# Output projection of the second layer as seven products of half matrices, with left sums on VectorE and right sums on GpSimd

## The reference

```python
        else:
            h = x @ b_w_in[j]
            u, v, qm = jnp.split(h, [SGU_WIDTH, 2 * SGU_WIDTH], axis=-1)
            mix = causal_chunk_sgu(jax.nn.gelu(u), jax.nn.gelu(v), sgu_ln_g[j], sgu_ln_b[j],
                                   sgu_w_s[j], sgu_b_s[j])
        mo = memory_attention(qm.reshape(B, S, N_MEM_HEADS, HEAD_DIM), mk, mv).reshape(B, S, MEM_WIDTH)
        y = jnp.concatenate([mix, mo], axis=-1) @ w_out[i]
        x = layer_norm(DN_ALPHA * x + y, ln_mix_g[i], ln_mix_b[i])
        f = (jax.nn.silu(x @ w_gate[i]) * (x @ w_up[i])) @ w_down[i]
        x = layer_norm(DN_ALPHA * x + f, ln_ffn_g[i], ln_ffn_b[i])
```

## Time and profile before

| what | value |
|---|---|
| median of 3 runs | 2175.58 us (2175.55 to 2175.66) |
| profiled execution: its span, first to last instruction | 2173.8 us |
| what the runs' time has beyond that span | 1.8 us |
| TensorE busy / weight loads | 99% / 84% of the span |
| VectorE, ScalarE, GpSimd busy | 62%, 43%, 60% |
| mean granted TensorE clock | 0.997 of full |

### The profile page before, as it was taken

How to read it: one execution, slowest core, us unless ns; L and a number is a source line. 1 busy time by engine, 2 the same in 40 slices (tenths; PEclk the granted TensorE clock), 3 DMA queues, 4 the chain that set the end, 5 groups by cost and what they waited for, 6 DMA issues and landing times.

```text
span 2173.8 us, 32211 instructions
## 1 busy us (share of the span) xinstructions
PE 2143.0 (99%) x10960; PEld 1822.5 (84%) x10960; DVE 1343.5 (62%) x2447; ACT 929.9 (43%) x1751; POOL 1301.1 (60%) x863
## 2 busy tenths in 40 slices
PE   8999999999999999999999999999999999999997
PEld 7888888888888888888888899988878888888885
DVE  5655565655875555566547747657866555555567
ACT  5655555632533343443324753213444333333323
POOL 5221222374498777777773793424698777777764
PEclk9999999999999999999999999999999999999998
DMA  5211111142012111111131311201012111111111
GB/s 176 74 53 46 58 49 59 44 136 59 20 59 59 58 51 55 54 51 55 46 96 49 102 48 47 78 22 57 20 59 68 55 57 54 58 58 58 54 62 79
DMA packets 164701, 132.64 MB, mean 61 GB/s; under 512 B 12656, under 2 KB 148464, under 8 KB 164592
## 3 DMA queue, kind: packets, MB, share of 16 engines
q1 hardware_dynamic: 149568, 115.36, 17.6%
q10 hardware_dynamic: 15024, 15.83, 2.5%
HBM read 122.78 MB, written 4.19 MB: 58 GB/s over the span
## 4 chain that ended last, share of the span: by engine, by line
PE 91%; DVE 4%; POOL 3%; issue 1%; ACT 1%; DMA 0%; ACTq 0%; DVEq 0%; POOLq 0%
PE ps L361 27%; PE ps L363 27%; PE ps L362 27%; PE ps L716 3%; PE ps L744 2%; PE ps L745 2%; PE ps L703 2%; PE ps L704 1%; POOL Rl L1896 1%; PE ps L1149 1%; POOL XR L1333 1%; PE ps L1063 1%; DVE V L2418 1%; POOL raw L1918 0%; DVE T2l L1606 0%
## 5 line engine op out<-in xcount | busy, mean ns | idle before, releaser
L2102 DVE TENSOR_TENSOR XR<-XR,ps 128x512 f32<-128x512 f32 x504 | 338.8, 686 | 215.4 <-PE ps L363 215.4
L318 POOL TENSOR_TENSOR Wh<-raw,zcol 128x1024 fp32r<-128x1024 f32 x76 | 144.7, 1904 | 466.6 <-PE ps L363 389.5
L1896 POOL TENSOR_TENSOR Rl<-raw,Rh 128x512 fp32r<-128x512 f32 x216 | 285.6, 1324 | 121.4 <-ACT Rh L1740 118.9
L361 PE MATMUL ps<-XTh,Wh 128*128 128x512 f32 x608 | 248.6, 409 | 0.5 <-DVE bQl L922 0.4
L363 PE MATMUL ps<-XTh,Wl 128*128 128x512 f32 x608 | 238.2, 392 | 0.0
L362 PE MATMUL ps<-XTl,Wh 128*128 128x512 f32 x608 | 237.8, 391 | 0.0
L361 PE MATMUL ps<-XTh,Rh 128*128 128x512 f32 x576 | 224.3, 389 | 3.3 <-POOL Rl L1896 3.3
L362 PE MATMUL ps<-XTl,Rh 128*128 128x512 f32 x576 | 224.1, 389 | 0.0
L363 PE MATMUL ps<-XTh,Rl 128*128 128x512 f32 x576 | 224.1, 389 | 0.0
L1740 ACT ACTIVATE Rh<-raw 128x512 fp32r<-128x512 f32 x216 | 135.8, 630 | 167.7 <-PE ps L363 143.6
L361 PE MATMUL ps<-Wh,XTh 128*128 128x256 f32 (+1 forms) x576 | 192.0, 333 | 0.0
(11 more groups left out here) (302 smaller groups left out, 5572.4 us busy)
## 6 DMA issues: line engine op xcount, KB each, us to landing
raw<-in_w_up SPq DMA_DIRECT2D x44, 512.0 KB, 3.8
raw<-in_w_gate SPq DMA_DIRECT2D x72, 256.0 KB, 2.9
rows<-in_w_down SPq DMA_DIRECT2D x36, 512.0 KB, 3.7
raw<-in_a_w_in SPq DMA_DIRECT2D x20, 512.0 KB, 3.8
raw<-in_w_out SPq DMA_DIRECT2D x16, 512.0 KB, 3.7
raw<-in_b_w_in SPq DMA_DIRECT2D x15, 512.0 KB, 3.8
B<-in_c_bias SPq DMA_DIRECT2D x12, 512.0 KB, 3.7
raw<-in_w_mem_kv SPq DMA_DIRECT2D x8, 512.0 KB, 3.9
```

The costliest lines, as they stand in the source:

```text
L318: nc.gpsimd.tensor_tensor(high, raw[:, turn, :], zcol[:, 0:1].to_broadcast([P, UNIT]), ALU.add).then_inc(high_done, 1)
L361: nc.tensor.matmul(dst, wh, xh, start=first, stop=False, skip_group_check=onto)
L1896: nc.gpsimd.tensor_tensor(Rl[(w - 1) % 4][:, :], source(w), Rh[(w - 1) % 4][:, :].bitcast(F32), ALU.subtract).then_inc(gs[L]("low"), 1)
L2102: nc.vector.tensor_tensor(x, x, bank(4 + i), ALU.add).then_inc(gf[L]("added"), 1)
```

## The change

The 1024x1024 times 1024x1024 product is cut in halves in each direction and made as seven products of halves (Winograd's form) instead of eight. The left matrix needs four sums, S1 to S4, of quarters of the activations; the right one four, T1 to T4, of quarters of `w_out`. Each quarter is stored as two pieces (`c` = 0, 1) of 128x1024 values per partition row, so each sum is two instructions, and so are its high part and its low part.

```diff
+    BLOCKS = [(b, c) for b in ("11", "12", "22") for c in range(2)]
+    BLOCKS = [BLOCKS[n] for n in (0, 1, 2, 4, 3, 5)]
...
+    PLACE = ((0, 1), (1, 1), (0, 1), (0, 0), (1, 0), (1, 1), (0, 1))
+    OPENS = (0, 1, 5)
+    FIRST_BANK = (0, 4, 0, 0, 0, 4, 4)
+    TO = ((1, 0), (1, 0), (1, 1), (0, 1), (0, 0), (0, 1), (1, 1))
+    LEFT_SUMS = [(n, c) for c in range(2) for n in ("S3", "S1", "S2")] + [("S4", c) for c in range(2)]
+    LEFT_OF = {2: "S2", 3: "S3", 5: "S1", 6: "S4"}
+    SUM_OF = {2: "T2", 3: "T3", 4: "T4", 5: "T1"}
...
+    def seven_pe(pe, d, units=range(4)):
...
+        for i in units:
+            b = FIRST_BANK[d] + i
...
+            else:
+                pe.wait_ge(*go[1]("added", 4 * {2: 0, 3: 2, 4: 3, 5: 1, 6: 5}[d] + i + 1))
...
+            for c in range(2):
+                if i == 0:
+                    pe.wait_ge(*right_split("low", d, c))
+                    if d in LEFT_OF:
+                        pe.wait_ge(*left_split("low", LEFT_OF[d], c))
+                rh, rl = right_of(d, c)
+                for k in range(2):
...
+                    mm = three(bank(b), XTh[:, at_k, ts], XTl[:, at_k, ts], rh[:, k * 512:k * 512 + 512],
+                               rl[:, k * 512:k * 512 + 512], opens and (c, k) == (0, 0), (c, k) == (1, 1), onto=not opens)
+            mm.then_inc(go[1]("product"), 1)
...
+    def left_high7_act(act, n, c):
...
+        nc.scalar.activation(left_place(XTh, d, c), left_source7(n, c), ACT.Copy).then_inc(g7("left_high"), 1)
...
+    def right_sum7_pool(pool, n, c):
...
+        nc.gpsimd.tensor_tensor(dst, x, y, op).then_inc(g7("right_sum"), 1)
+    def right_high7_act(act, d, c):
...
+        if d < 3:
+            act.wait_ge(sem("uproj_product"), (2 * NT, 3 * NT, NT)[d])
+        else:
+            act.wait_ge(*go[1]("product", 4 * (d - 2)))
...
+    def seven_pool(pool):
+        for c in range(2):
+            right_low7_pool(pool, 0, c)
+        for n, c in RIGHT_SUMS[:4]:
+            right_sum7_pool(pool, n, c)
+        for d in (1, 2):
+            for c in range(2):
+                right_low7_pool(pool, d, c)
+        for c in range(2):
+            right_sum7_pool(pool, "T4", c)
+        for c in range(2):
+            right_low7_pool(pool, 3, c)
+        for c in range(2):
+            right_sum7_pool(pool, "T1", c)
+        for d in (4, 5, 6):
+            for c in range(2):
+                right_low7_pool(pool, d, c)
...
+    def seven_sums_dve(dve):
+        for n, c in LEFT_SUMS[:6]:
+            left_sum7_dve(dve, n, c)
+        for c in range(2):
+            left_low7_dve(dve, "S2", c)
+        seven_dve(dve, 0, range(2, 4))
+        for c in range(2):
+            left_low7_dve(dve, "S3", c)
+        seven_dve(dve, 1)
+        for c in range(2):
+            left_low7_dve(dve, "S1", c)
+        for n, c in LEFT_SUMS[6:]:
+            left_sum7_dve(dve, n, c)
+        seven_dve(dve, 2)
...
+    def tile_at(n):
+        return (n + 4) % NT
...
         for n in range(7, 3 * NT):
             gelu(n)
+            if n == 2 * NT + 1:
+                for c in range(2):
+                    right_high7_act(act, 0, c)
             if n >= 2 * NT + 2:
                 turn(n - 2 * NT - 2)
-        turn(NT - 2)
-        turn(NT - 1)
+        for d in (1, 2):
+            for c in range(2):
+                right_high7_act(act, d, c)
+            turn(NT - 3 + d)
...
+            else:
+                seven_pe(pe, 0, range(2, 4))
+                for d in range(1, 6):
+                    seven_pe(pe, d)
+                seven_pe(pe, 6, range(2))
+                for j in range(4):
+                    row_turn(pe, go[1], j, None)
+                seven_pe(pe, 6, range(2, 4))
```

More of the change, by code:

```diff
@@ L254, in build, with part_of @@
     VSLOTS = (6, 7, 0, 1, 2, 3)
[L255 to L261, removed]
+    OUT_PARTS = [(0, 1, 2), (3, 4, 5), (6, 7)]
+    CLOSE = len(OUT_PARTS) - 1
+    def part_of(k):
+        return next(c for c, ks in enumerate(OUT_PARTS) if k in ks)
     def letters(p):
@@ new lines, in build, with summed, left_summed, left_split @@
+    LEFT_OF = {2: "S2", 3: "S3", 5: "S1", 6: "S4"}
+    RIGHT_SUMS = [(n, c) for c in range(2) for n in ("T3", "T2")] + [(n, c) for n in ("T4", "T1") for c in range(2)]
+    SUM_OF = {2: "T2", 3: "T3", 4: "T4", 5: "T1"}
+    B_OF = ("11", "21", "11", "12", "21", "12", "22")
+    def summed(t, h):
+        d = (1, 6)[h] if t >= 4 else (4, 5)[h]
+        return go[1]("added", 4 * d + t % 4 + 1)
+    def left_summed(n, c):
+        return g7("left_sum", LEFT_SUMS.index((n, c)) + 1)
+    def left_split(part, n, c):
+        return g7(f"left_{part}", LEFT_SPLITS.index((n, c)) + 1)
@@ new lines, in right_summed, with right_split, block_f32, block_landed @@
+    def right_summed(n, c):
+        return g7("right_sum", RIGHT_SUMS.index((n, c)) + 1)
+    def right_split(part, d, c):
+        if d == 4:
+            return {"high": high_done, "low": split_done}[part], U_B21 + c + 1
+        return g7(f"right_{part}", 2 * (d - (d > 4)) + c + 1)
+    def block_f32(b, c):
+        return raw[:, (U_B21 + c) % RS, :] if b == "21" else blocks_f32[b, c][:, :]
+    def block_landed(b, c):
+        if b == "21":
+            return raw_landed[(U_B21 + c) % RS], 16 * ((U_B21 + c) // RS + 1)
+        return BLOCK_LANDED[b, c]
@@ new lines, in seven_dve @@
+    def seven_dve(dve, d, units=range(4)):
+        row, half = TO[d]
+        for i in units:
+            dve.wait_ge(*go[1]("product", 4 * d + i + 1))
+            x = XR[:, 4 * row + i, half * 512:half * 512 + 512]
+            p = bank(FIRST_BANK[d] + i)
+            if d in FIRST_TOUCH:
+                nc.vector.scalar_tensor_tensor(x, x, ALPHA, p, ALU.mult, ALU.add).then_inc(go[1]("added"), 1)
+            else:
+                dve.wait_ge(*go[1]("added", 4 * TO.index(TO[d]) + i + 1))
+                nc.vector.tensor_tensor(x, x, p, ALU.add).then_inc(go[1]("added"), 1)
@@ new lines, in seven_norm_dve @@
+    def seven_norm_dve(dve):
+        g = go[1]
+        for i in range(4):
+            seven_dve(dve, 5, (i,))
+            if i:
+                rstd_dve(dve, g, i - 1)
+            stats_dve(dve, g, None, i, range(1, 2))
+        seven_dve(dve, 6, (0,))
+        rstd_dve(dve, g, 3)
+        stats_dve(dve, g, None, 4, range(1, 2))
+        rstd_dve(dve, g, 4)
+        seven_dve(dve, 6, (1,))
+        for j in range(2):
+            row_dve(dve, g, j)
+        seven_dve(dve, 6, (2,))
+        for j in range(2, 4):
+            row_dve(dve, g, j)
+        stats_dve(dve, g, None, 5, range(1, 2))
+        seven_dve(dve, 6, (3,))
+        rstd_dve(dve, g, 5)
+        for j in range(4, KT):
+            row_dve(dve, g, j)
+        stats_dve(dve, g, None, 6, range(1, 2))
+        stats_dve(dve, g, None, 7, range(1, 2))
+        rstd_dve(dve, g, 6)
+        rstd_dve(dve, g, 7)
@@ L2212, in ready @@
                 pe.wait_ge(sem("mix_low"), (3, 5, 7)[c])
[L2213 to L2220, removed]
+        acc_pe(pe, go[0], c, U_OUT + ks[0], lambda i, t: out_lhs(ks[i], t), [out_rhs(k) for k in ks], ready,
+               after=norm_pe_after(pe, go[0], c) if c == CLOSE else None, tiles=tiles, halves=halves)
     def out_piece_pe(pe, n, k):
         t, h = n // 2, n % 2
-        pe.wait_ge(split_done, U_OUT[0] + k + 1)
+        pe.wait_ge(split_done, U_OUT + k + 1)
         pe.wait_ge(sem("mix_low"), k + 1)
@@ L2688, in _ @@
         pool.wait_ge(*gsg("v_low", NG))
-        for u in range(U_U + 4, U_FFN[1]):
+        for u in range(U_U + 4, U_B21):
             split(pool, u)
+        seven_pool(pool)
         ffn_units(1)
@@ L2749, in _ @@
                 sgu_pe(pe)
[L2751 to L2752 removed]
+            if L == 0:
+                for c in range(len(OUT_PARTS)):
+                    out_pe(pe, c, range(3, NT) if c == 0 else range(NT))
+            else:
+                seven_pe(pe, 0, range(2, 4))
[5 more added lines that the diff above has]
+                seven_pe(pe, 6, range(2, 4))
+                for j in (4, 5):
+                    row_turn(pe, go[1], j, None)
             ffn_pe(pe, L, 0, True, False)
```

290 lines of the change are left out of this document (216 added, 74 removed).

## The result

The changed kernel takes 2185.45 us (median of 4 runs, 2184.27 to 2185.56), the kernel before 2175.62 us (4 runs) on the same chip. The ratio is 1.0044, with a 95% interval of 1.0031 to 1.0056: slower by 9.8 us. The forecast was 2185.8 us, in a range of 2171 to 2192.

What follows compares the result with a forecast made beforehand. The prediction took TensorE, busy 99% of the span, as the bound. Its terms, -10.9 + 4.0 + 2.3 + 12.4 + 0.5 + 1.9 = +10.2 us, gave 2185.8 us, in a range of 2171 to 2192.

Steps and rivals of the forecast that it cites:

- Matmuls, -10.9: Second output projection: 384 matmuls become 336, and the 48 removed save 0.2267 us each on PE, -10.9 us.
- A pair costs 3.35: One POOL and one DVE instruction of 128x1024, both reading SBUF, largely take turns: 3.35 us together, between 2.38 and 3.52.
- Turns, +4.0: Turns of U tiles before the projection: DVE's short SBUF instructions wait out six POOL instructions over three tiles, +4.0 us.
- Before d2, +2.3: Ahead of product d2: DVE's left sums meet three POOL instructions, so S2's first low part comes late, +2.3 us.
- Before d3, +12.4: Ahead of product d3: DVE's addition of d2 stands behind five instructions that each meet one of POOL's, +12.4 us.
- Before d4, +0.5: Ahead of product d4: DVE's addition of d3 is queued behind S4's low parts and four statistics, +0.5 us.
- The clock, +1.9: After the wait ahead of d3: PE's clock has fallen, and sixteen matmuls lose 0.12 us each, +1.9 us.
- steps 1, 2 and 5: The turns (+4.0 us), the wait ahead of d2 (+2.3) and the clock restart (+1.9), whose ends were said to give the range.
- step 3: The wait ahead of product d3 for DVE's late addition of d2: +12.4 us, ends 1.3 and 13.7.
- kinder turns: Rival: DVE gets several instructions between two of POOL's, or the layout lets them overlap; 2166 to 2168 us, chance 0.20.
- Only d3's wait: Rival: the turns keep their slack and the clock stays up, so +2.0 us, 2177.6 us; chance 0.12.
- More: Rival: the clock falls at d2 too, pairs cost 3.52 us, the row turns miss; 2189 to 2193 us, chance 0.12.

Runs made afterwards that it cites:

- e2: Changed kernel with POOL's right sums and low parts made on only 64 of 1024 columns, work left out, all waits kept: 2164.61 us.
- best1: Changed kernel with POOL, ACT and DVE work reordered around PE's three waits, and POOL's low parts of d3 held back by one wait: 2164.55 us.
- e6: Changed kernel with 42 unread matmuls added on PE in the wait ahead of product d3: 2183.39 us.
- e4: Changed kernel with POOL's T3 sums ahead of d0's low parts and ACT's d0 high parts two GELUs earlier: 2181.19 us.
- e1: Changed kernel with DVE's additions of d2 moved ahead of S1's low parts and the S4 sums: 2179.41 us.
- e5: Changed kernel with the edits of e1 and e4, plus d3's low parts ahead of POOL's T4 sums and its high parts first on ACT: 2177.44 us.
- best1_nohold: best1 without the one wait that holds POOL's low parts of d3 until DVE has made S2's low parts: 2173.14 us.

## Why the prediction was right

The mechanism stood, and its terms, taken on the profiled execution (span +8.7 us), come out so:

- *Matmuls, -10.9.* Right. e2 and best1 show it alone: spans of 2162.8 and 2162.9 us against 2173.8.
- *A pair costs 3.35.* Right within 0.07: 6.71 for two of POOL's and 3.35 and 3.36 for DVE's as durations, 3.28 for DVE's from start to start. The Trainium skill, "SBUF — State Buffer", section "Who interferes with whom", has the two exclude each other for the whole instruction. By the costs of rows 8 that is 3.52, an estimate. The rule holds in kind, but about 0.2 us of each pair overlapped.
- *Turns, +4.0.* Slightly too large: d0 starts at 1419.88 against 1416.39, +3.5, and the turn after its second unit is 3.5 later too (3.6 with the 0.1 us by which the two traces are shifted). The waits are 0.45, 1.36 and 1.34; the step had 0.7, 1.6 and 1.6.
- *Before d2, +2.3.* Measured 2.1. The four sums took 11.21, which is three pairs (10.05) and one alone (1.14), as the step has it.
- *Before d3, +12.4.* Measured 11.8. All five instructions met one of POOL's, as was said: one inside the 4.57, two in the 6.66, then 3.35 and 3.36. The error of 0.6 isn't in the count: about 0.3 of it is in the price of five pairs (3.28 and not 3.35), and the rest in that DVE began the stretch earlier (1444.57 against 1445.0).
- *Before d4, +0.5.* This step failed, though by little (by its own figures it comes to 1479.9 and not 1479.7, so to +0.7). There is no such wait in the changed kernel. e6 shows it once the clock stays up: a gap of 0.28. The sum added it to the restart's cost, but the two cover each other, since a PE at half pace reaches d4 later than DVE does.
- *The clock, +1.9.* Measured 2.0: nine matmuls in 4.0 us, half pace. e6 takes it away and gives 1.2 us by the profiled spans and 2.1 by the medians. That the size fits so well is in part luck: it was taken from transposes at the program's start, and other restarts in the runs lost from 1.3 to 2.8 us (last section).

The sum is -10.9 + 3.6 + 2.1 + 11.8 + 0.0 + 2.0 = +8.6, against 8.7. The medians differ by 9.8, so the forecast of +10.2 was helped by chance: its terms were 1.5 too large for the execution with the profile, which was the fastest of four.

The forecast's own range isn't what it says it is made of: the ends of steps 1, 2 and 5, added up, give 2177.6 to 2190.3 and not 2181 to 2191. And the 13.7 at the upper end of step 3 counts the three pairs of step 2, which would lengthen d2's wait and not d3's.

Of the rivals, "kinder turns" needed DVE to get several instructions between two of POOL's. No trace shows that; only e2, where POOL's were short, and best1, where they were kept away, reach its time. "Only d3's wait" fails on both of its conditions, since the turns waited 3.1 us and the clock fell. "More" was partly right in a place that costs nothing: the clock did fall at d2, in the profiled executions of e4 and e6, but the longer wait before d3 hid it. What was covered at nothing stayed so: POOL's weight passes for the FFN begin at 1492.02 (forecast "about 1490"), and PE doesn't wait for them.

```profile
1492.02 1.90 POOL L324 TENSOR_TENSOR Wh<-raw,zcol 128x1024 fp32r<-128x1024 f32 x1 [5.32 <-PE ps L369]
```

## What to carry to other kernels

Trading TensorE work for elementwise sums isn't priced by the busy shares of the helpers: first find out, on one row beside the other, whether their instructions run side by side or take turns. If they take turns, count each meeting at its price, and look at which result the bottleneck needs next; a helper whose work is early can hurt more than one whose work is late. Put work that doesn't take part in the turn (here additions out of PSUM) between the instructions that do, and hold a helper back where its work would meet a more urgent one: here one such wait was worth 8.6 us.

## What was not expected of the hardware

- How long PE runs at half pace after a wait isn't the same each time. Counted in matmuls that start 0.4 us or more apart, it is from 1467.67 to 1471.68 in the changed kernel (4.0 us, after a wait of 11.8), 5.7 us in e1 (wait 6.0), 4.9 in e4 (wait 10.2), 5.7 in e5 (wait 10.5), 2.7 in best1_nohold (wait 6.3). That is 1.3 to 2.8 us lost, and it doesn't grow with the wait. Whether it makes the times of one kernel spread wasn't tried. The times don't say so: the runs of best1, with no wait in the stage, lie within 0.15 us and those of the changed kernel within 1.3, but the 25 runs of the kernel before, with no wait in the stage either, lie within 1.5.
- A wait of 2.1 us lowered the clock in some executions (e4, e6) and not in others (the changed kernel, e1), each read from one profiled execution. In those where it fell, it fell after PE had started again: the rows of 0.63 begin 0.9 us after e4's restart at 1441.80.
- VectorE has no column for standing in such a turn: 3.35 us and 1.22 us are both "busy". What gave it away was the same instruction's duration at two places.
